# Low parts of u tiles by an adding DMA, and one-hots six steps earlier

## What is computed

```
...
def peer(x, w_q, sub_keys, u, v):
    ...
        s_top, i_top = lax.top_k(s, PEER_TOPK)
        cand = s_top[:, :, 0, :, None] + s_top[:, :, 1, None, :]
        ...
        best, pos = lax.top_k(cand, PEER_TOPK)
        eidx = jnp.take_along_axis(cand_idx, pos, axis=-1)
        g = jax.nn.softmax(best, axis=-1)
        ug = jnp.take(u, eidx, axis=0)
        vg = jnp.take(v, eidx, axis=0)
        h = jax.nn.gelu(jnp.einsum('td,thkd->thk', xb, ug).astype(jnp.float32), approximate=False)
        return jnp.einsum('thk,thkd->td', (g * h).astype(x.dtype), vg)
```

## Time and profile before

| | |
|---|---|
| Time, median of 3 runs (lowest to highest) | 1615.29 us (1611.36 to 1616.25) |
| The profiled execution's own time | 1614.49 us |
| Its span | 1612.7 us |
| PE busy | 1577.1 us (98%) |
| DVE busy | 1281.4 us (79%) |
| ACT busy | 630.0 us (39%) |
| POOL busy | 517.4 us (32%) |
| PE waits for low parts by DVE (L1437 for L1265) | 13.8 us, 27 times |
| Clock granted to PE, mean | 0.998 |

### The profile page before, as it was taken

One profiled execution on the slowest core, in us unless ns is written; L12 is line 12 of the kernel. 1 busy time (PEld: TensorE's weight loads), 2 busy tenths in 40 slices (PEclk: granted clock), 3 DMA queues, 4 the chain that ended last, 5 costly groups with the idle time before them and its releaser, 6 DMA issues.

```text
span 1612.7 us, 24488 instructions
## 1 busy us (share of the span) xinstructions
PE 1577.1 (98%) x9566; PEld 1389.2 (86%) x9566; DVE 1281.4 (79%) x2390; ACT 630.0 (39%) x996; POOL 517.4 (32%) x261
## 2 busy tenths in 40 slices
PE   9999999999999999899999989999999999999998
PEld 7897977888989999889999988888888888888886
DVE  3024366246899999999998789999999999999997
ACT  5324445523223333345455333333333434333332
POOL 4433232361235778421010233333332232222200
PEclk9999999999999999999999999999999999999999
DMA  5342112133124669699998999999999999999972
GB/s 203 142 149 84 58 53 79 60 135 147 53 92 138 186 199 303 214 331 315 350 354 256 291 420 398 392 396 394 387 391 422 413 409 415 392 391 410 399 297 78
DMA packets 141633, 427.05 MB, mean 265 GB/s; under 512 B 11344, under 2 KB 73040, under 8 KB 120272
## 3 DMA queue, kind: packets, MB, share of 16 engines
q1 hardware_dynamic: 118224, 274.47, 46.9%
q0 software_dynamic: 23296, 151.04, 23.8%
HBM read 378.77 MB, written 46.14 MB: 263 GB/s over the span
## 4 chain that ended last, share of the span: by engine, by line
PE 62%; DVE 31%; DMA 3%; issue 2%; ACT 1%; POOL 0%; SPq 0%; DVEq 0%
PE bank L1437 19%; PE bank L1439 18%; PE bank L1438 18%; DVE wlo L1265 5%; DVE acc L1311 4%; DVE uvb L1273 4%; PE bank L1743 3%; DMA raw<-in_u 2%; DVE idx L1179 1%; DVE idx L1171 1%; DVE val L1170 1%; DVE val L1178 1%; DVE tmp L1172 1%; DMA raw<-in_uv 1%; DVE uvb L1283 1%
## 5 line engine op out<-in xcount | busy, mean ns | idle before, releaser
L1437 PE MATMUL bank<-xhi,whi 128*128 128x352 f32 (+1 forms) x1408 | 491.2, 349 | 22.8 <-DVE wlo L1265 13.8
L1439 PE MATMUL bank<-xhi,wlo 128*128 128x352 f32 (+1 forms) x1408 | 480.8, 341 | 0.0
L1438 PE MATMUL bank<-xlo,whi 128*128 128x352 f32 (+1 forms) x1408 | 480.7, 341 | 0.0
L714 POOL DMA_INDIRECT uvb<-in_uv,eidx x128 | 200.2, 1564 | 571.9 <-DVE acc L1311 422.3
L896 ACT ACTIVATE whi<-raw 128x1024 fp32r<-128x1024 f32 x255 | 268.7, 1055 | 207.1 <-PE bank L1439 148.8
L1437 PEld LDWEIGHTS bank<-xhi,whi 128*128 128x128 f32 x1408 | 265.2, 188 | 50.6 <-DVE wlo L1265 25.1
L1265 DVE TENSOR_TENSOR wlo<-raw,whi 128x1024 fp32r<-128x1024 f32 x215 | 261.9, 1219 | 44.6 <-ACT whi L896 44.4
L1437 PE MATMUL bank<-whi,ahi 128*128 128x512 f32 x762 | 296.7, 389 | 0.0
L1438 PE MATMUL bank<-wlo,ahi 128*128 128x512 f32 x762 | 296.7, 389 | 0.0
L1439 PE MATMUL bank<-whi,alo 128*128 128x512 f32 x762 | 296.5, 389 | 0.0
L1439 PEld LDWEIGHTS bank<-xhi,wlo 128*128 128x128 f32 x1408 | 265.3, 188 | 15.5
(11 more groups left out here) (225 smaller groups left out, 1860.8 us busy)
## 6 DMA issues: line engine op xcount, KB each, us to landing
raw<-in_u SPq DMA_DIRECT2D x128, 512.0 KB, 6.3
raw<-in_uv SPq DMA_DIRECT2D x127, 512.0 KB, 9.2
g_scratch<-stage SPq DMA_DIRECT2D x48, 512.0 KB, 6.9
gl<-g_scratch SPq DMA_DIRECT2D x32, 768.0 KB, 9.6
raw<-in_w_in SPq DMA_DIRECT2D x22, 1024.0 KB, 4.9
h_scratch<-hout SPq DMA_DIRECT2D x96, 192.0 KB, 5.3
hl<-h_scratch SPq DMA_DIRECT2D x24, 768.0 KB, 11.0
raw<-in_w_q SPq DMA_DIRECT2D x6, 1024.0 KB, 4.7
```

The source lines that it names most:

```text
L714: nc.gpsimd.indirect_dma_start(out=uvb[:, r % UVB, :], out_offset=None, in_=a["uv"][:, :], in_offset=bass.IndirectOffsetOnAxis(ap=eidx[:, ...
L1437: mm(out, lh, rh, start=first, stop=False)
L1438: mm(out, lh, rl, start=False, stop=False)
L1439: return mm(out, ll, rh, start=False, stop=last)
```

## The change

For u tiles 6 to 37 POOL's subtraction goes. After the high part, ACT writes the raw tile once more with a scale of -1 into the low part's buffer, rounded the same way, so that it holds the negated high part. POOL then issues a DMA that reads the raw tile from DRAM again and adds it to that buffer. PE waits for this DMA (`low_added`); SP's reload of a raw slot waits for ACT's second copy (`tile_neg`). Tiles 0 to 5 stay with POOL's subtraction. DVE makes low parts from tile 38 on and enters its loop at step 34. The steps at which DVE does the weights, picks, `dots_c` and one-hots move down by 4 to 7 steps (one-hots from 42 to 84, before 48 to 90), the first ten gathers are issued from tile 17 to 29 in pairs every three tiles, and six pairs of gathered experts are summed before step 97, where there were four; so 27 are summed at steps 97 to 155, where there were 29.

```diff
-POOL_ONLY = 40
-EXP_STEP = 39
-NORM_STEP = 43
-PICKS_TILE = 42
-PICKS_STEP = 46
-HOT0, HOT1, HOT2 = 48, 86, 90
-C_STEPS = [41, 42, 43, 44, 45, 47] + [49 + 3 * i for i in range(NCP - 6)]
-C_TILE, C_STEP = 80, 80
+ADD_FIRST, ADD_END = 6, 38
+DVE_FIRST = 34
+EXP_STEP = 34
+NORM_STEP = 37
+PICKS_TILE = 37
+PICKS_STEP = 41
+HOT0, HOT1, HOT2 = 42, 80, 84
+C_STEPS = [34, 35, 36, 38, 39, 40] + [43 + 3 * i for i in range(NCP - 6)]
+C_TILE, C_STEP = 76, 76
...
-GL_FIRST, GL_SECOND = 95, 99
+GL_FIRST, GL_SECOND = 94, 98
...
-GATHER_TILE = 25
+GATHER_TILE = 16
...
-SUM_STEPS = [89, 91, 93, 95] + [97 + i * 59 // 29 for i in range(29)] + [156 + i * 94 // 31 for i in range(31)]
+SUM_STEPS = [84, 86, 88, 90, 92, 94] + [97 + i * 59 // 27 for i in range(27)] + [156 + i * 94 // 31 for i in range(31)]
...
         def wait_low(engine, s):
 
-            if s < POOL_ONLY:
+            if s < ADD_FIRST:
                 engine.wait_ge(low_pool, s + 1)
+            elif s < ADD_END:
+                engine.wait_ge(low_added[s % 4], 16 * len([t for t in range(ADD_FIRST, s + 1) if t % 4 == s % 4]))
             else:
-                engine.wait_ge(low_dve, s + 1 - POOL_ONLY)
+                engine.wait_ge(low_dve, s + 1 - ADD_END)
...
+                elif ADD_FIRST <= s - 4 < ADD_END:
+                    sp.wait_ge(tile_neg, s - 4 - ADD_FIRST + 1)
...
-            for s in range(POOL_ONLY):
+            def tile_add(s):
+
+                pool.wait_ge(tile_neg, s - ADD_FIRST + 1)
+                nc.gpsimd.dma_start(wlo4[:, slot4(s), :], a["u"][s], accum_op=ALU.add).then_inc(low_added[s % 4], 16)
+
+            for s in range(ADD_FIRST):
                 tile_low(s)
+            for s in range(ADD_FIRST, ADD_END):
+                tile_add(s)
...
-                if GATHER_TILE < s <= GATHER_TILE + UVB:
-                    gather_u(s - GATHER_TILE - 1)
+                if s > GATHER_TILE and (s - GATHER_TILE) % 3 == 1 and (s - GATHER_TILE) // 3 < UVB:
+                    gather_u((s - GATHER_TILE) // 3)
...
                 nc.scalar.activation(hi, r, ACT.Copy).then_inc(tile_hi, 1)
+                if ADD_FIRST <= n < ADD_END:
+                    nc.scalar.activation(lo, r, ACT.Copy, scale=-1.0).then_inc(tile_neg, 1)
...
-            for s in range(POOL_ONLY, 2 * NT):
-                tile_low(s)
+            for s in range(DVE_FIRST, 2 * NT):
+                if s >= ADD_END:
+                    tile_low(s)
```

More of the change, by code:

```diff
@@ L423, in program @@
         tile_hi, low_pool, low_dve = sem("tile_hi"), sem("low_pool"), sem("low_dve")
+        tile_neg = sem("tile_neg")
+        low_added = [sem(f"low_added{i}") for i in range(4)]
         h_done, h_gelu = sem("h_done"), sem("h_gelu")
```

## The result

The change made the kernel slower: 1620.97 us (median of 7 runs, 1619.74 to 1623.6) against 1615.14 us before (7 runs, 1610.56 to 1616.25), a ratio of 1.0048 with a 95% interval of 1.0037 to 1.0058. 1603 and faster was forecast; the time is in the range, but by rival 1.

A forecast was written before the change was run, and what follows sets the result against it. TensorE, busy 98% of the span, was taken as the bound, so only its lost time could be gained. From 1614.5 us, -11.0 (hand-over) - 10.7 (fused stage) + 4 (before it) + 6 (adds) gave 1602.8, said as 1603; range 1596 to 1632.

The forecast's parts named there:

- rival 1: Tiles 6 to 37: DMA engines become the bound and TensorE waits for adds; 1630 to 1645 us, chance 0.27.
- The exclusion of GpSimd and VectorE: Expert selection: GpSimd's subtractions and VectorE's operations block each other; removing them takes 26.9 us off the selection.
- The hand-over: Tiles 30 to 40 and first one-hots: TensorE's waits for late low parts and one-hots go, 11.0 us gained.
- The two sums of the fused stage: Fused stage, bound by VectorE: two of 29 sums move ahead of it, making it 10.7 us shorter.
- the stretch before it: Before the fused stage: four more 1 MB gathers cost between 1.5 and 10.4 us, taken as 4.
- The rest of the change: All terms but the adding transfers: hand-over, fused stage and the stretch before it, together a gain of 17.7 us.
- The adding transfers: Tiles 6 to 37: adds are hidden by landing time but load the DMA engines; cost taken as 6 us.
- the bounds: Cost of adds in tiles 6 to 37: 0 by landing time, 48 us if an add costs twice a plain transfer.
- the turn to a loss: Tiles 6 to 37: the change becomes a loss once an add takes 1.63 us of DMA engine time.
- Rivals 2 and 3: 2: gathers before the fused stage and adds cancel the gain, 1613 us, 0.17; 3: both fit, 1596, within the forecast's case.
- issuing adds holds VectorE up: Selection: 32 issues on GpSimd of about 1 us would take back all 26.9 us; called a small chance.

## Why the prediction was wrong

**What held.** All mechanisms but one came as they were worked out, though not in every size. The exclusion of GpSimd and VectorE ended: without adds the selection ends and VectorE's next work starts at 628.1 (635.9 predicted), the first one-hot comes at 659.37 (660.2). That the second figure fits is luck. The selection became 34 us shorter, not 26.9, since the sum left out smaller groups that were held up as well (L1214 with 64 columns, 491 ns for 221 now, eight times; L1206, 822 for 300, four times; L1388 and L1241: 7 us in all); and VectorE then idled 6.87 us for ScalarE's exponentials, which the sum didn't have. The hand-over was to be worth 11.0 us. Six steps with one-hots more now lie before tile 48; from tile 42 to 80 such a step takes 189.20 / 38 = 4.98 us, 1.14 above a plain one, so they bring 6.8 us there; so the stretch from 38 to 48, which is 1.46 us shorter, gained 1.46 + 6.8 = 8.3 after the change; without adds it gained 1.2 + 6.8 there and 0.9 before tile 38, 8.9. The two sums of the fused stage were to give 10.7 and give 9.0. For the stretch before it I took a loss of 4; the stretch from 84 to 99 is 6.9 us shorter, but four one-hot steps of 5.29 us instead of 3.84 left it, 5.8 us, so 1.1 were gained there. In the kernel of before the two sums cost 4.4 alone; that the free steps that now lie there paid for them is my reading, and no run separates it. The rest of the change is thus worth 8.3 + 1.1 + 9.0 = 18.4 us with the adds, and the run without them measured 19, for 17.7 predicted.

**What failed** is the step "The adding transfers": its term of 6 us measured 25.5, of which before lost 0.9 anyway; 24.6 - 18.4 is the 6 us by which the kernel is slower. The choice between the bounds was wrong. I took the gather of the earlier trace rows, 6.6 us to land, as the row nearest to an add, and by landing time the add was hidden; in truth it lands in 8.8 us before the gathers start, just within the 8.9 us that it had, and in 10.5 beside them, beyond it. Adds of after from 565 to 660 us:

```profile
wlo<-in_u POOLq DMA_DIRECT2D x19, 512.0 KB, 10.5
```

What was missed is how long it holds the DMA engines: 2.64 us where a plain transfer in its place holds them 1.64. That makes the hardware queue's loads late (3.9 to 14.5 us), and with them ScalarE's input to the next add. Beside this loop the sum had no term for the clock, and 9 of the 25.5 us are TensorE slower after waits.

The Trainium skill's rule, which stood against my choice (Collectives: The Full Stack, The bandwidth ceiling: the fold count and why AG ≠ RS ≠ AR), says that the addition costs no time but its two source reads halve the rate. The trace agrees in kind: 2.64 against 1.64 us is 1.6 times the plain price, and in the run with half the adds and the gathers apart 0.424 x 32 / (2.29 / 0.524) = 3.1 us is 1.9 times, though the plain price was taken beside another load. That the add holds the engines this long is shown; that the second read is the reason is the rule's, and no run separates it. DMA of the run with half the adds and the gathers apart, from 523 to 555 us:

```profile
q0 software_dynamic: 622, 2.29, 42.4%
```

**Rival 1** had the place and the sign, at 0.27, but not the size. With 2.64 us its formula gives (2.36 + 2.64 - 3.84) x 32 + 13 = 50 us of loss, and 25.5 came; with the plain copy's 1.64 it gives 18, and 6.5 came. So the turn to a loss is not at 1.63 us: the plain copy at 1.64 still leaves 0.9919. The engines' times don't add up as a hard limit. The share reaches 1.03 to 1.06 in these windows, and a tile's load and h store, which held 0.605 x 32 / 8 = 2.42 us before, hold 0.376 x 32 / 6.2 = 1.9 us for each 0.72 MB beside the adds. Rivals 2 and 3 fell with the price of an add; that issuing adds holds VectorE up is refuted by its groups.

Still open: how much of the dearer add is the second read, and how much waiting for memory within a packet's time. The view counts both.

## What to carry to other kernels

A transfer that is free by its landing time can still be the dearest one by the engine time that it takes from others: price it by its queue's share of the engines, over a stretch that has it, and look at what lands late beside it. A DMA that adds is not a plain transfer, and one plain copy in its place tells the two apart in one run. When work moves off an engine, move the steps that depend on it by what the new end allows and no more: two steps here decided between 1609.87 and 1601.2 us.

## What the runs showed of the hardware

- An adding DMA of 512 KB held the engines 2.64 us, a plain one in its place 1.64; with an SBUF source the add held them 2.74, and 3.1 where only every second tile was added.
- A wait of TensorE costs more than its length where the granted clock falls after it: 5.91 us became 8.5, and 3.2 became 6.9.
- GpSimd's subtraction in four pieces takes 4 x 884 ns = 3.5 us on the mean, for 2.65 in one.
